# Gate products in fp32r, gelu behind the next splits, and matmul runs of sixteen in a two-block fp32 transformer step

## What is computed

```python
def peer(x, wq, keys1, keys2, u, v):
    ...
    v1, i1 = lax.top_k(s1, PEER_TOPK)
    v2, i2 = lax.top_k(s2, PEER_TOPK)
    ...
    top_s, pos = lax.top_k(cand_s, PEER_TOPK)
    expert = jnp.take_along_axis(cand_i, pos, axis=-1).reshape(t, -1)
    gate = jax.nn.softmax(top_s.astype(jnp.float32), axis=-1).astype(x.dtype).reshape(t, -1)
    ...
        z = jnp.einsum('cd,ced->ce', xc, u[ec])
        act = jax.nn.gelu(z, approximate=False) * gc
        return jnp.einsum('ce,ced->cd', act, v[ec])
```

## Time and profile before

| | us |
|---|---|
| median of 3 runs | 2789.57 (2788.06 to 2791.62) |
| the profiled execution | 2789.84 |
| its span | 2787.9 |
| PE busy in the span | 2744.4 (98%) |
| DVE busy | 1818.3 (65%) |
| ACT busy | 1409.1 (51%) |
| POOL busy | 342.3 (12%), nearly all of it between 1490 and 1725 us |

### The profile page before, as it was taken

The page is one execution under the profiler, slowest core; times in us unless marked ns, Lnnn a source line. Parts: engine busy times, 40 slices in busy tenths (PEclk is TensorE's granted clock), DMA queues, the critical chain, the costliest instruction groups (busy, mean ns, idle before and its releaser), DMA issues.

```text
span 2787.9 us, 48242 instructions
## 1 busy us (share of the span) xinstructions
PE 2744.4 (98%) x14688; PEld 2366.5 (85%) x14688; DVE 1818.3 (65%) x2903; ACT 1409.1 (51%) x2067; POOL 342.3 (12%) x438
## 2 busy tenths in 40 slices
PE   8999999999999999999999999999999999999998
PEld 6888878888888888888888999888888888888887
DVE  6666665668986666579995666666665555555555
ACT  5455545556665444466655544555554444444444
POOL 0000000000001110011126996000000000000000
PEclk9999999999999999999999999999999999999999
DMA  6544455564554444555555445666665555555564
GB/s 244 190 156 162 150 169 187 177 218 159 173 179 160 158 155 140 195 183 192 191 195 176 156 158 162 214 214 209 214 206 196 195 190 195 192 192 195 191 238 158
DMA packets 153554, 514.76 MB, mean 185 GB/s; under 512 B 17056, under 2 KB 33696, under 8 KB 152480
## 3 DMA queue, kind: packets, MB, share of 16 engines
q1 hardware_dynamic: 131904, 480.44, 52.2%
q10 hardware_dynamic: 21600, 33.70, 3.4%
HBM read 501.49 MB, written 12.58 MB: 184 GB/s over the span
## 4 chain that ended last, share of the span: by engine, by line
PE 73%; issue 21%; POOL 2%; DVE 2%; ACT 1%; DMA 0%; POOLq 0%; SPq 0%; DVEq 0%; ACTq 0%
PE bank L509 21%; PE bank L514 11%; PE bank L2249 8%; PE bank L2251 8%; PE bank L2250 8%; PE bank L547 3%; PE bank L549 3%; PE bank L548 3%; PE bank L2224 2%; POOL big L634 2%; DVE w_lo L469 1%; PE bank L492 1%; PE bank L494 1%; PE bank L493 1%; PE bank L2082 0%
## 5 line engine op out<-in xcount | busy, mean ns | idle before, releaser
L469 DVE TENSOR_TENSOR w_lo<-raw,w_hi 128x1024 fp32r<-128x1024 f32 x904 | 1105.7, 1236 | 796.2 <-ACT w_hi L460 791.0
L460 ACT ACTIVATE w_hi<-raw 128x1024 fp32r<-128x1024 f32 x904 | 951.4, 1059 | 933.0 <-PE bank L2251 373.2
L509 PE MATMUL bank<-act,w_hi 128*128 128x512 f32 x3840 | 980.7, 397 | 5.4 <-ACT big L984 1.9
L509 PEld LDWEIGHTS bank<-act,w_hi 128*128 128x128 f32 x3840 | 692.0, 189 | 136.2 <-issue 7.8
L514 PEld LDWEIGHTS bank<-act,w_lo 128*128 128x128 f32 x3840 | 523.3, 190 | 39.4 <-DVE w_lo L469 0.8
L514 PE MATMUL bank<-act,w_lo 128*128 128x256 f32 x3840 | 535.1, 282 | 0.1
L2249 PE MATMUL bank<-w_hi,expert_act 128*128 128x512 f32 x1008 | 392.2, 389 | 0.1
L2250 PE MATMUL bank<-w_lo,expert_act 128*128 128x512 f32 x1008 | 392.1, 389 | 0.0
L2251 PE MATMUL bank<-w_hi,expert_act 128*128 128x512 f32 x1008 | 392.1, 389 | 0.0
L2249 PEld LDWEIGHTS bank<-w_hi,expert_act 128*128 128x128 f32 x1008 | 189.3, 188 | 39.6 <-DVE cst L525 0.5
L2251 PEld LDWEIGHTS bank<-w_hi,expert_act 128*128 128x128 f32 x1008 | 189.3, 188 | 39.3
(11 more groups left out here) (308 smaller groups left out, 2603.3 us busy)
## 6 DMA issues: line engine op xcount, KB each, us to landing
raw<-in_stream SPq DMA_DIRECT2D x904, 512.0 KB, 3.3
big<-in_ukv ACTq DMA_DIRECT2D x16, 512.0 KB, 4.6
z_kept<-cst ACTq DMA_DIRECT2D x64, 128.0 KB, 3.1
cst<-z_kept ACTq DMA_DIRECT2D x64, 128.0 KB, 3.8
big<-in_x SPq DMA_DIRECT2D x2, 1024.0 KB, 9.6
big<-in_rows ACTq DMA_DIRECT2D x2, 1024.0 KB, 8.3
big<-in_rg_w ACTq DMA_DIRECT2D x1, 2048.0 KB, 11.0
x_kept<-big ACTq DMA_DIRECT2D x1, 2048.0 KB, 6.7
```

The costliest lines, as they stand in the source:

```text
L460: act.activation(w_hi[:, s, :], raw[:, s, :], ACT.Copy).then_inc(hi_ready, 1)
L469: dve.tensor_tensor(w_lo[:, s, :], raw[:, s, :], w_hi[:, s, :].bitcast(F32), ALU.subtract).then_inc(lo_ready, 1)
L509: pe.matmul(bank[:, :], w_hi[:, s, kk * P:(kk + 1) * P], act2[:, k, :, :].rearrange("p a n -> p (a n)"), start=(k == 0), stop=False)
```

## The change

Line numbers of the changed kernel differ by about ten and more; the names are the same.

1. `halves_out` runs the 16 wide matmuls of both units first and then the 16 narrow ones, in every halved block. `unit_done` of unit 0 now comes after the first eight narrow ones, behind all wide ones.
2. In `wqu` and `u_decode` ACT's `early` is cut in two: `keep_early` (the copy) stays where it was, and `save_early` (gelu and store) stands one block later, behind the next pair's splits.
3. The gate products: `hot` becomes fp32r; the weighted table of a token becomes 2 x 128 wide (its high and its low part, made by one SCALAR_TENSOR_TENSOR on DVE with two inputs in SBUF), so one fp32r matmul of 256 columns replaces the f32 one. All four weighted tables of a turn are made at its start, ahead of both low splits. ACT takes the low halves of two tokens at a time to `G`, and DVE then adds the high halves (`add_gates`, two a turn).
4. `u_gates` is now 32 turns of 2 pairs and 8 tokens: one whole pair to four tokens, with the gate products between the narrow matmuls of unit 0 and of unit 1. It has 64 pairs, `u_late` has 32, and 32 of the multiplications by gates (with ACT's loads back) are spread over the first 32 turns of `v`, two in each.

```diff
-         ("wqu", 4 * PH), ("u_decode", 2 * PH), ("u_gates", S // 8), ("u_late", NB // 2), ("v", NB)]
-EARLY = NB // 2
+         ("wqu", 4 * PH), ("u_decode", 2 * PH), ("u_gates", S // 4), ("u_late", NB // 4), ("v", NB)]
+EARLY = 3 * NB // 4
+LATE = NB - EARLY
...
+            for u in units:
+                if u and between:
+                    between()
                 pe.wait_ge(lo_ready, 2 * pair + u + 1)
                 for kk in range(8):
...
                 ahead(split_hi, act, "wqu", h, 4, 3)
-                early(pair_of("wqu", h, 4, 3), h, 1, h * 4 + 3, 4)
+                save_early(h, 0, h * 4 + 2)
+                keep_early(pair_of("wqu", h, 4, 3), 1, h * 4 + 3, 4)
...
             def early_turn(i):
                 for n in range(2):
                     ahead(split_hi, act, "u_decode", i, 2, n)
-                    early(pair_of("u_decode", i, 2, n), i + PH, n, i * 2 + (4 * PH + n), 2)
+                    save_early(i + (PH - 1 + n), 1 - n, i * 2 + (4 * PH + n - 1))
+                    keep_early(pair_of("u_decode", i, 2, n), n, i * 2 + (4 * PH + n), 2)
...
+            with act.Fori(0, S // 8) as i:
                 for n in range(2):
                     ahead(split_hi, act, "u_gates", i, 2, n, units=(0,))
-                    keep_gates(0)
+                    for half in range(2):
+                        act.wait_ge(hot_used[2 * half + 1], i * 2 + n + 2)
+                        act.activation(G[:, :, bass.ds(i * 8 + (4 * n + 2 * half), 2)],
+                                       GATE_BANKS[n][half].rearrange("p (t a b) -> p a b t", t=2, a=2)[:, 1, :, :],
+                                       ACT.Copy).then_inc(gate_low, 1)
                     ahead(split_hi, act, "u_gates", i, 2, n, units=(1,))
...
+            def add_gates(i, n):
+                for half in range(2):
+                    dve.wait_ge(gate_low, i * 4 + (2 * n + half + 1))
+                    dest = G[:, :, bass.ds(i * 8 + (4 * n + 2 * half), 2)]
+                    high = GATE_BANKS[n][half].rearrange("p (t a b) -> p a b t", t=2, a=2)[:, 0, :, :]
+                    dve.tensor_tensor(dest, dest, high, ALU.add).then_inc(gate_kept[n], 1)
...
+                        dve.scalar_tensor_tensor(
+                            out=weighted[:, s, :, :], in0=iota.unsqueeze(1).broadcast_to([P, 2, P]),
+                            scalar=first_index[:, bass.ds(tok, 1)],
+                            in1=slot_t[:, 1:3, bass.ds(tok, 1)].broadcast_to([P, 2, P]),
+                            op0=ALU.is_equal, op1=ALU.mult).then_inc(hot1, 1)
+                    ahead(split_lo, dve, "u_gates", i, 2, n)
                     add_halves(dve, GZ[:, n, :], banks[2 + n], block_of("u_gates", i, 2, n))
+                    add_gates(i, n)
...
+            def four_tokens(i, n):
+                pe.wait_ge(gate_kept[n], i * 2 + 1)
+                pe.wait_ge(hot1, i * 8 + (4 * n + 4))
+                pe.wait_ge(hot2, i * 8 + (4 * n + 4 + 1))
+                for s in range(4):
+                    pe.matmul(GATE_BANKS[n][s // 2][:, (s % 2) * S:(s % 2 + 1) * S], hot[:, s, :],
+                              weighted[:, s, :, :].rearrange("p a b -> p (a b)"), start=True, stop=True)\
+                      .then_inc(hot_used[s], 1)
```

More of the change, by code:

```diff
@@ L83 @@
 _n = 0
-for _name, _count in [("conv", 4 * CONV_J), ("rnn", 2 * KT), ("heads", 2 * H2), ("u_gates", S // 8),
-                      ("u_late", NB // 2)]:
+for _name, _count in [("conv", 4 * CONV_J), ("rnn", 2 * KT), ("heads", 2 * H2), ("u_gates", S // 4),
+                      ("u_late", LATE)]:
     HALVED[_name] = _n
@@ L162, in build @@
             pass
-        hot = sb("hot", [P, 2, 4, P])
+        weighted = sb("weighted", [P, 4, 2, P], F32R)
+        with nc.sbuf_tensor("below_hot", [P, CONST["causal"][0]], F32), \
+                nc.sbuf_tensor("hot", [P, 4, P], F32R) as hot:
+            pass
         cst = sb("cst", [P, CONST_W])
@@ L498, in block_of, with halves_out @@
             return i * per + (HALVED[part] + k)
-        def halves_out(pe, pair, odd, bank, units=(0, 1), fills=None):
+        def halves_out(pe, pair, odd, bank, units=(0, 1), between=None, fills=None):
             for u in units:
@@ L513, in halves_out @@
                     k = 8 * u + kk
-                    mm = pe.matmul(bank[:, 0:S], w_lo[:, s, kk * P:(kk + 1) * P], act_hi[:, k, :], start=False,
-                                   stop=(k == KT - 1))
+                    mm = pe.matmul(bank[:, 0:S], w_lo[:, unit_slot(odd, u), kk * P:(kk + 1) * P], act_hi[:, k, :],
+                                   start=False, stop=(k == KT - 1))
                 mm.then_inc(unit_done, 1)
@@ L984, in copy_halves, with keep_early, save_early @@
                 act.activation(dest, bank[:, :], ACT.Copy).then_inc(copied, 1)
-            def early(pair, b2, n, block, before):
+            def keep_early(pair, n, block, before):
                 copy_halves(Z_HALVES[:, n, :], banks[2 + n], pair, block, before)
+            def save_early(b2, n, block):
                 act.wait_ge(z_saved[n], b2 * 16 + 1)
@@ L994, in early, with router_turn @@
                    .then_inc(z_saved[n], 16)
-            with act.Fori(0, PH) as h:
+            def router_turn(h, first=False):
                 def keep_query(a):
@@ L1008, in _ @@
                 keep_query(0)
+                if not first:
+                    save_early(h - 1, 1, (h - 1) * 4 + 3)
                 ahead(split_hi, act, "wqu", h, 4, 1)
@@ L1012, in _ @@
                 ahead(split_hi, act, "wqu", h, 4, 2)
-                early(pair_of("wqu", h, 4, 2), h, 0, h * 4 + 2, 4)
+                keep_early(pair_of("wqu", h, 4, 2), 0, h * 4 + 2, 4)
                 keep_scores(1)
                 ahead(split_hi, act, "wqu", h, 4, 3)
-                early(pair_of("wqu", h, 4, 3), h, 1, h * 4 + 3, 4)
+                save_early(h, 0, h * 4 + 2)
+                keep_early(pair_of("wqu", h, 4, 3), 1, h * 4 + 3, 4)
+            router_turn(0, first=True)
+            with act.Fori(1, PH) as h:
+                router_turn(h)
             def early_turn(i):
@@ L1810, in expert_lo @@
                                   expert_hi_t[:, n, :].bitcast(F32), ALU.subtract).then_inc(el_ready, 1)
-            with dve.Fori(0, EARLY // 2 - 1) as i:
+            with dve.Fori(0, LATE // 2 - 1) as i:
                 late_turn(i)
```

99 lines of the change are left out of this document (53 added, 46 removed).

## The result

The changed kernel takes **2817.70 us** (median of 4 runs, 2814.93 to 2818.28) against 2789.69 (4 runs, 2788.06 to 2791.62) for the kernel before: ratio 1.0095, 95% interval 1.0083 to 1.0108 (the quotient of the two medians is 1.0100). That is 28.0 us slower, where +12.9 was forecast. The sign, and the loop in `u_gates` that causes most of it, were as forecast. The size was not, and ahead of `u_gates` a gain was forecast where a loss came.

A forecast was written before the change was run, and what follows sets the result against it. PE, 98% busy, bounded the kernel; afterwards a 6.85 us loop ordered by DVE's list would bind u_gates. Stages +19.3, runs of sixteen -2.9, early gelu -3.5 gave +12.9: 2802.5 us, range 2773 to 2825.

The forecast's parts named there:

- the loop in `u_gates`: Chain from products through ACT's and DVE's splits, additions and four weighted tables back to products: 6.85 us; PE needs 6.04.
- L1787: Rival: u_gates weighted tables cost what this line's operation costs; loop 0.44 us shorter, 2775 us; chance 0.08.
- The rival in which the loop doesn't bind: In u_gates handovers hide and a turn is PE's own 6.04 us; 2751.5 us; chance 0.10.
- ahead of `wqu`, runs of sixteen: Each halved pair ahead of u_gates saves 0.02 us by sixteen wide then sixteen narrow; 144 pairs, 2.9 us.
- `wqu` and `u_decode`, early gelu: Later gelu frees ACT's bank copy from POOL's sum; PE waits of 1.70 and 1.75 go, saving 3.5 us.
- first wide to first products: Start of u_gates: split, gelu and store, copy, POOL's sum, index copy and four tables take 7.4 us.
- half clock there: The wait at u_gates' first products brings a stretch at half clock, 1.7 us lost.
- 63 turns: The binding loop in u_gates repeats 63 times at 6.85 us, 431.6 us.
- 32 pairs of `u_late`: The remaining pairs in u_late take 5.56 us each, 177.9 us.
- the two waits that were forecast to go: PE waits of 1.70 us (for L984) and 1.75 us (for L991) ahead of u_gates should vanish, 3.5 us.
- DVE is held by POOL: Rival: each unit 1 split in u_gates waits out a 0.60 us POOL table; loop 7.45, 2840 us; chance 0.10.

The follow-up runs named there:

- the last kernel: Changed kernel with low_half before ACT's unit 1 split, DVE's tables between add_halves and unit 1's split, copy before gelu in wqu/u_decode: 2750.81 us, ratio 0.9859.
- two experiments: Kernel before with runs of sixteen outside u_gates: 2790.97 against 2790.11 us; changed kernel with runs of eight outside u_gates: 2817.10 us.

## Why the prediction was right and wrong

**Right: what the loop in `u_gates` is, and that it binds.** Every link of the chain is in the timeline in the forecast order, PE's wait ends with L1825 in every turn, and adding 1.07 us or taking 0.71 away moved the turn by that length, but for the tenth in the next point. The tables stand 0.39 apart and are 0.474 long, forecast 0.40 and 0.48 from the row nearest in kind; L1787 would have been the wrong row. The rival in which the loop doesn't bind is refuted, but its time (2751.5) is what the last kernel reaches, with another order.

**The sum, term by term**, of the profiled executions (span +28.6):

| term | forecast | measured | from |
|---|---|---|---|
| ahead of `wqu`, runs of sixteen | -2.9 with `wqu` and `u_decode` | +0.5 | first wide matmul of `wqu`, 1201.25 and 1201.73 |
| `wqu` and `u_decode`, early gelu | -3.5 | +3.3 | first wide of `u_gates`, 1482.24 and 1485.99, less the above |
| first wide to first products | 7.4 | 5.6 | 1485.99 to 1491.57 |
| half clock there | 1.7 | 0 | granted 1.00 from 1484 to 1494 |
| 63 turns | 63 x 6.85 | 63 x 6.976 | the turn above |
| 32 pairs of `u_late` | 32 x 5.56 | 1.2 more | 5.56 each, but one wait of 0.69 at 1944.55 |

From +12.9 this goes by +3.4, +6.8, -1.8, -1.7, +8.0 and +1.2 to +28.8. These are the rows of the two starts and of `u_late` in the kernel after:

```profile
1201.73 1.65 PE L518 MATMUL bank<-act,w_hi 128*128 128x512 f32 x6 [0.63 <-DVE act L1181]
...
1485.99 3.92 PE L518 MATMUL bank<-act,w_hi 128*128 128x512 f32 x16 [1.61 <-ACT cst L1006]
...
1491.57 0.74 PE L2271 MATMUL bank<-weighted,hot 128*128 128x256 f32 x4 [0.71 <-POOL hot L667]
...
1944.55 1.65 PE L518 MATMUL bank<-act,w_hi 128*128 128x512 f32 x6 [0.69 <-DVE cst L537]
```

**Wrong, first: the early gelu.** The failing step is "the copy itself, since gelu and store now stand ahead of it: split end 1.2 after the pair, plus 1.16, plus 0.58, 2.9 against the 5.58". It put gelu's wait for POOL's sum at nothing; the one length of that sum that the prediction used was the 1.47 of a calm place. In `u_decode` the sum was held for 8.39 us, with DVE at two-input operations all the while, and the timeline of the kernel before had this to be read, in rows that the prediction didn't use:

```profile
1418.40 6.23 POOL L634 TENSOR_TENSOR big<-big 128x256 f32<-128x256 f32 x1 [3.98 <-ACT big L984]
...
1424.66 0.42 ACT L991 ACTIVATE cst<-big 128x256 f32<-128x256 f32 x1 [6.34 <-POOL big L634]
```

The copy became later by the wait that it was to be freed from, and in the changed kernel a stretch at half clock came with it. With the copy first the kernel before gained 3.2 us, though not by the two waits that were forecast to go.

**Wrong, second: the turn.** 0.13 us a turn was missing, 8.0 in all, the largest term. The steps that were too short are DVE's split to add_halves, 1.24 for 1.15, and the additions, 1.04 for 0.99. For the first I had let the rival "DVE is held by POOL" stand apart, at 0.60, and put nothing of it into the sum; the truth was 0.09. The Trainium skill (SBUF — State Buffer, Who interferes with whom) has both engines lock each other out for a whole instruction. The trace agrees on POOL, whose tables took 1.03 on average instead of 0.60, and whose sum took up to 8.39 instead of 0.73, which is several instructions of DVE and not one. On DVE it disagrees in `u_gates`, where beside a POOL table of 0.60 the split grew from 1.23 to 1.37 at most, and agrees ahead of it, where beside POOL's sum a split took 1.76 for 1.22. The prediction had looked at splits in `u_gates` alone; the kernel before has this as well:

```profile
1433.00 1.16 POOL L634 TENSOR_TENSOR big<-big 128x256 f32<-128x256 f32 x1 [3.98 <-ACT big L984]
...
1433.48 1.76 DVE L469 TENSOR_TENSOR w_lo<-raw,w_hi 128x1024 fp32r<-128x1024 f32 x1
```

**Wrong, third: the runs of sixteen.** The distances between matmuls are shorter, as forecast, but the gain of some 1 to 3 us is below what these runs can tell (two experiments, both zero). In the changed kernel the stretch at half clock at 1192 us is longer (0.57 granted of 1192 to 1200, 0.79 before), but costs nothing: the 32 matmuls that stand there take 5.95 us in both kernels, and the first wide one of `wqu` comes 6.57 behind their start in both. Of the kernel before, and of after:

```profile
1194.67 5.95 PE L1885 MATMUL bank<-cst,big 128*128 128x128 f32 x32 [4.60 <-DVE big L1196]
```
```profile
1195.16 5.95 PE L1936 MATMUL bank<-cst,big 128*128 128x128 f32 x32 [4.59 <-DVE big L1225]
```

Other stretches lie at other places in the two executions: in the changed kernel one near 1104 us, which the kernel before has near 577. The stretch of 1100 to 1110, of the kernel before and of after:

```profile
1100.00:1110.00 10.00, 8.02 (x36) 6.32 (x35) 5.83 (x10) 2.93 (x5) 0.72 (x1) 1.00 0.35 108
```
```profile
1100.00:1110.00 10.00, 8.02 (x29) 6.21 (x28) 4.39 (x8) 2.78 (x4) 0.72 (x1) 0.83 0.44 131
```

PE is 1.1 us ahead of the kernel before at 1100 and 0.5 behind at 1110. So where such a stretch falls moves a place in one execution by as much as the gain looked for. It is not tied to the runs of sixteen: the kernel before with the copy first has it near 1104 too, and the last kernel, with runs of sixteen, near 577.

**Two terms that were too high.** First wide to first products took 5.6 for 7.4, since gelu and store stand ahead of the first wide matmul and not behind it: the copy starts 0.33 after it (1486.32), where the sum had 1.26 + 1.16. And the stretch at half clock there did not come, with a wait of 0.71 for the 2.8 forecast. These two errors, 3.5 us, hid part of what was missing; that the total came as near as 15 us is in so far luck.

**What stays open.** When a wait of PE comes with a stretch at half clock. The wait for the copy near 1435 us came with 16 wide matmuls in 6.36 to 6.71 us in all eight kernels that have it and runs of sixteen, with 8 in 3.60 (usually 2.11) in the changed kernel with runs of eight, and with none in the kernel before with the gelu moved, whose 8 took 2.11. So the runs of sixteen may have a part in it that the times don't show; two kernels without them are too few to tell. Undoing the gelu's order alone gave back 2.4 us and the copy first 7.2. Most of that difference is in waits: with the old order PE still waits 1.82, 2.28 and 1.60 us (for the copy, the gelu and POOL's tables) between 1425 and 1490, with the copy first only the 2.10 for the gelu. Why a stretch falls near 577 us in one kernel and near 1104 in another was not settled either, nor where the shorter distances of the runs of sixteen are lost again.

## What to carry to other kernels

When an edit changes the order of instructions in a loop with several engines, write each engine's list for one turn and follow every cycle through them, not only the one that looks longest: an operation that one engine puts off (here add_halves) holds whatever waits for it on another engine, with that engine's next turn behind it. Put off what is needed latest (add_gates, needed two turns on) rather than what somebody waits for. A step that waits for a slow or disturbed engine goes last on its own engine, behind the step that frees a bank, and is costed from its longest row, not from a calm one.

## What the runs showed of the hardware

- DVE's two-input operations held one POOL sum of 256 columns for 6.23, 6.93 and 8.39 us, through several DVE instructions in a row; undisturbed it takes 0.73. DVE lost at most 0.14 us of a split to POOL's tables (1.37 against 1.23, in `u_gates`), but 0.54 beside POOL's sum (1.76 against 1.22, at 1433.48 us of the kernel before).
- In the changed kernel a wait of 3.7 us on PE came with a stretch at 1.2 GHz, in which 16 wide matmuls took 6.65 us instead of 3.82, so the wait cost nearly twice its length. That does not follow from the wait alone: behind a wait of 3.45 us in the kernel before with the gelu moved, the clock was 1.00 and 8 wide matmuls took 2.11.
- The fp32r products of 256 columns stand 0.12 us apart, as narrow matmuls do, though both their inputs were just written by other engines: (0.57 - 0.10) / 4, where 0.10 is what a run after a wait takes longer.
